# An expert layer's down weights, issued from the ScalarE queue instead of the SyncE queue

## What is computed

```
def block_ffn(args):
    xblk, e = args
    return (jax.nn.silu(xblk @ w_g[e]) * (xblk @ w_u[e])) @ w_d[e]

yb = lax.map(block_ffn, (xb, blk_e)).reshape(P, D)
```

## Time and profile before

| what | value |
|---|---|
| median of 3 runs | 4818.37 us (4810.97 to 4830.34) |
| time of the profiled execution | 4811.15 us |
| its span, first to last instruction | 4809.1 us |
| busy over the span: TensorE, VectorE, ScalarE, GpSimd | 76%, 37%, 19%, 1% |
| mean granted TensorE clock | 0.872 of full |
| bytes moved by DMA | 485.17 MB, mean 101 GB/s |
| experts' loads in it | 96 of 2048 KB each |
| first expert load issued, end of the last down product | 1516.03 us, 2041.70 us |

### The profile page before, as it was taken

The page is one execution under the profiler, slowest core; times in us unless marked ns, Lnnn a source line. Parts: engine busy times, 40 slices in busy tenths (PEclk is TensorE's granted clock), DMA queues, the critical chain, the costliest instruction groups (busy, mean ns, idle before and its releaser), DMA issues. The chain is left out here.

```text
span 4809.1 us, 70093 instructions
## 1 busy us (share of the span) xinstructions
PE 3634.8 (76%) x29962; PEld 2832.5 (59%) x29962; DVE 1793.0 (37%) x3421; ACT 924.6 (19%) x1532; POOL 54.4 (1%) x70
## 2 busy tenths in 40 slices
PE   4889959469964777738578655799989758778887
PEld 3678938347553344337238445688878645466677
DVE  4645543742242000054414245444410353344433
ACT  2154420122010111120001332211100212222211
POOL 0000000000000000000000000000000000000000
PEclk7989969789986999969689887899999879989888
DMA  4120006013414999934111000244420010012222
GB/s 150 42 101 4 4 30 180 13 46 97 131 62 177 423 423 423 391 106 133 41 44 62 3 1 27 59 113 118 120 77 25 24 38 1 18 49 70 66 64 81
DMA packets 376984, 485.17 MB, mean 101 GB/s; under 512 B 16311, under 2 KB 326104, under 8 KB 368513
## 3 DMA queue, kind: packets, MB, share of 16 engines
q1 hardware_dynamic: 367728, 459.59, 27.6%
q0 software_dynamic: 3856, 13.11, 0.7%
q10 hardware_dynamic: 5120, 8.39, 0.5%
HBM read 455.88 MB, written 25.18 MB: 100 GB/s over the span
## 5 line engine op out<-in xcount | busy, mean ns | idle before, releaser
L243 PE MATMUL banks<-leading,w_rest 128*128 128x512 f32 (+2 forms) x1920 | 716.1, 373 | 162.8 <-DVE w_rest L203 162.8
L243 PE MATMUL banks<-rest,w_leading 128*128 128x512 f32 (+2 forms) x1920 | 704.9, 367 | 0.0
L243 PE MATMUL banks<-leading,w_leading 128*128 128x512 f32 (+2 forms) x1920 | 703.1, 366 | 0.0
L243 PEld LDWEIGHTS banks<-leading,w_rest 128*128 128x128 f32 (+1 forms) x1920 | 374.4, 195 | 236.9 <-issue 97.2
L243 PE MATMUL banks<-w_rest,leading 128*128 128x256 f32 (+3 forms) x1332 | 395.3, 297 | 104.2 <-DVE w_rest L203 104.2
L203 DVE TENSOR_TENSOR w_rest<-w,w_leading 128x1024 fp32r<-128x1024 f32 (+4 forms) x304 | 280.8, 965 | 497.1 <-ACT w_leading L197 497.1
L243 PEld LDWEIGHTS banks<-leading,w_leading 128*128 128x128 f32 (+1 forms) x1920 | 374.0, 195 | 61.4
L243 PEld LDWEIGHTS banks<-rest,w_leading 128*128 128x128 f32 (+1 forms) x1920 | 375.0, 195 | 58.2
L197 ACT CAST w_leading<-w 128x1024 fp32r<-128x1024 f32 (+4 forms) x304 | 240.3, 838 | 846.6 <-DMA w<-in_w_in 458.3
L243 PE MATMUL banks<-w_leading,rest 128*128 128x256 f32 (+3 forms) x1332 | 390.7, 293 | 0.0
L243 PE MATMUL banks<-w_leading,leading 128*128 128x256 f32 (+3 forms) x1332 | 390.2, 293 | 0.0
(11 more groups left out here) (534 smaller groups left out, 4892.4 us busy)
## 6 DMA issues: line engine op xcount, KB each, us to landing
wg<-in_w_exp_gate SPq DMA_DIRECT2D x32, 2048.0 KB, 28.4
wu<-in_w_exp_up SPq DMA_DIRECT2D x32, 2048.0 KB, 28.4
wd<-in_w_exp_down SPq DMA_DIRECT2D x32, 2048.0 KB, 27.9
ws<-in_ada_w SPq DMA_DIRECT2D x96, 512.0 KB, 3.9
w<-in_w_in SPq DMA_DIRECT2D x41, 1024.0 KB, 5.4
w<-in_ffn_up SPq DMA_DIRECT2D x44, 512.0 KB
w<-in_ffn_up SPq DMA_DIRECT2D x88, 256.0 KB
ws<-in_w_ada SPq DMA_DIRECT2D x32, 512.0 KB, 3.9
```

The lines of the kernel that those rows point to most:

```text
L243: mm = nc.tensor.matmul(bank_of(r, kind, at), lhsT, rhs, start=(k == 0 and q == 0), stop=(k == kt - 1 and q == len(each) - 1))
```

## The change

The issue of the down weights leaves SyncE's loop. In ScalarE's loop it stands at the head of each block: a read of the block's expert, the same wait on `y_made_sem`, and the same DMA.

```
@@ -1753,8 +1753,6 @@
                         sp.dma_start(wg[u][:, :, :], a["w_exp_gate"][bass.ds(e, 1)].rearrange("o (p k) n -> p (o k) n", p=P)).then_inc(g_in_sem[u], 16)
                         sp.wait_ge(u_made_sem, 2 * it + u + 1)
                         sp.dma_start(wu[u][:, :, :], a["w_exp_up"][bass.ds(e, 1)].rearrange("o (p k) n -> p (o k) n", p=P)).then_inc(u_in_sem[u], 16)
-                        sp.wait_ge(y_made_sem, 2 * it + u + 1)
-                        sp.dma_start(wd[u][:, :, :], a["w_exp_down"][bass.ds(e, 1)].rearrange("o (k p) n -> p (o k) n", p=P)).then_inc(d_in_sem[u], 16)
 
             @block.gpsimd
             def _(pool):
@@ -1827,6 +1825,9 @@
                 with act.Fori(0, n) as it:
                     for u in range(2):
                         i = 2 * it + u
+                        e = act.value_load(m.expert_of[0:1, bass.ds(i, 1)], min_val=0, max_val=N_EXP - 1)
+                        act.wait_ge(y_made_sem, i + 1)
+                        act.dma_start(wd[u][:, :, :], a["w_exp_down"][bass.ds(e, 1)].rearrange("o (k p) n -> p (o k) n", p=P)).then_inc(d_in_sem[u], 16)
                         act.wait_ge(g_made_sem, i + 3)
                         nc.scalar.activation(b.sg[:, :], m.ps[:, 2, half(u)], ACT.Silu).then_inc(silu_sem, 1)
                         if u:
```

## The result

The changed kernel takes 5179.02 us (median of 4 runs, 5170.51 to 5186.12) against 4824.35 us for the kernel before (4 runs, 4810.97 to 4839.56). The ratio is 1.0737, 95% interval 1.0713 to 1.0762: 355 us slower. The forecast was 5147, with a range of 4950 to 5215.

The account below looks back on a forecast made before the run. The prediction took the experts to be bound by 16 full DMA engines. Its terms, 15.2 + 811.0 - 497.7 = 328.5 us, on the profiled 4811.15 us with 7.2 for the median, gave 5147 us, range 4950 to 5215.

Parts of the forecast that it names:

- The order on ScalarE puts the issue a block late: Head of ScalarE's block: load i issued only when block i-1 is finished, 3.06 us after the previous down product's last matmul.
- The first packets: Down load on ScalarE's queue: packets start 1.0 to 1.2 us after the issue, 1.2 taken, so at 4.26 us.
- When the gate and up loads arrive: Loads of block i+2 arrive at about 5 and 8.6 us, in the midst of the down load's transfer.
- All of both loads ahead of the down load: DMA engines: gate and up loads go through before the down load is done, 15.0 us for the three.
- One of the prediction's own signs of being wrong: Forecast is wrong if block i+2's gate and up loads land after block i's down load.
- Turns by the packet, whatever its size: DMA engines alternate queues packet by packet: 32 down turns against 16 larger packets; landing 18 us after issue; chance 0.80.
- Rival 1: DMA engines take longer turns or share by bytes: down load waits for one gate load, 4922 to 4991 us; chance 0.12.
- The down product at the lower clock: TensorE, idle some 12 us before it, takes 5.96 us instead of 3.65 for the down product.
- A block: Experts' stage, one block from down product to down product: 21.03 + 5.96 = 27.0 us instead of 16.13.
- The ends of the stage: First down product ends 15.2 us later; the last two blocks, without gate and up loads beside them, take 14.0 us each.
- Rival 2: Down load on its own queue is served at once, landing at 10.4 us; time stays at 4818 us; chance 0.04.
- Rival 3: Down load's issue meets busy engines, starts up to 4 us late: 116 us more, about 5260 us; chance 0.04.

Follow-up runs that it names:

- e11: Changed kernel with the value load ahead of the wait for y, issue still behind the stores, first down load ahead of all: 5082.15 us, ratio 1.0512 to the kernel before.
- e6: Changed kernel with value load ahead of the wait for y, issue ahead of the stores, first down load ahead of all: 4944.61 us; 62 us gain forecast, 234 measured.
- e3: Changed kernel with the down load in 8 packets of 16 KB per DMA engine instead of 32 of 4 KB: 4974.13 us, ratio 1.0292 to the kernel before.
- e5: Changed kernel with gate and up loads in 64 packets of 2 KB per DMA engine instead of 8 of 16 KB: 4949.08 us, ratio 1.0241 to the kernel before.
- e4b: Changed kernel with 26 extra matmuls into an unused bank ahead of TensorE's wait for the down load: 5137.84 us, ratio 1.0629 to the kernel before.
- e1: Changed kernel with the down load issued one block earlier, still on ScalarE's queue in 4 KB packets: 4900.86 us, ratio 1.0132 to the kernel before.

## Why the prediction was right, point by point

- **The order on ScalarE puts the issue a block late**: right. Issued 3.2 us after the previous down product, forecast 3.06.
- **The first packets** 1.2 us after the issue: right, some 1.0: issued at 1888.82, q10's packets run in the row that starts at 1889.6.
- **When the gate and up loads arrive**: wrong in size, about 5 and 8.6 us forecast. The gate load is issued at 3.6 and moves its first packets at 7.3 us, 3.6 us after the issue and not 1.2, and by then the engines are at work for q10. It left the sum alone, since in either case all of both loads goes through before the down load is done, but by a narrow margin and so in part by luck: 231 down packets, 14.4 per engine, were ahead of the gate load, not 5, and with over 16 the up load would no longer have been through, as in e11 and e6. The same mistake is why e6 came out at four times its forecast.
- **All of both loads ahead of the down load**: right to 3 packets. One of the prediction's own signs of being wrong, the up load landing after the down load, did come up, by a hair: in the block shown the down load lands at 1862.03 + 17.5 = 1879.5 and the up load at 1865.80 + 13.9 = 1879.7. In the next it is the other way round, 1907.9 and 1907.8. The load is waited for as forecast either way.
- **Turns by the packet, whatever its size**: right, 223 to 237 in the changed kernel, one for one from the gate load's first packets on, and e3 and e5 show that the packet size sets the time. Landing after 18.2 us, forecast 18. Rival 1 wanted 13 us, and falls with its sharing by bytes. Its longer turns were quoted from the Trainium skill (page "DMA: Bandwidth & Descriptors", section "Queues, rings and completion order"). The round robin there agrees with these rows. The length of the turn doesn't: that section has an engine drain a whole packet of typically 9 to 17 descriptors before it switches, and here it was one packet of the rows, as the half microseconds behind 1893.0 show. The landing alone would not have told: with turns of 8 or 9 packets the down load, with 18 left per engine, would also have let both loads through.
- **The down product at the lower clock**: 5.96 us forecast, 180.2 us / 32 = 5.63 measured. e4b gives it back, 2 us a block.
- **A block**: 27.0 forecast, 27.29 measured. 29 times 0.29 us are 8 of the 32 us by which the forecast was low.
- **The ends of the stage**: forecast 15.2 us for the first block; from the first load's issue to the end of the first down product it is 1558.91 - 1512.56 = 46.35 us, against 27.96 before: 18.4. The last two blocks took (2381.35 - 2350.39) / 2 = 15.5 us each, not 14.0; 1.7 of these 3 us are the first one's down product, 5.35 us at the lower clock. Together 6 us more. Stage 343 us against 328.5.
- **The rest**, 17 of the 32 us, lies outside the stage or in which runs are compared. Nothing in the change explains it; that stretch varies by as much between kernels that leave it alone, as said above, and why was not followed.
- Rival 2 (its own queue serves it at once) needed 70% of the engines; it had 86% for 3.3 us and then 19.8%. e6 comes near it, and even there a block takes 19.6 us. Rival 3 fell with the 1.0 us to the first packets.

## What to carry to other kernels

A load on a queue of its own overtakes the backlog of the other queue only at a packet for a packet, so small packets beside large ones get the small share; a load that is needed soon belongs ahead of the others in their queue, or on its own with packets as large as theirs, or clearly ahead of them in time. When a DMA's issue moves to a compute engine, read what that engine waits for just before it: here the wait for the previous block's result took away the block's lead that the double buffer had given. And where a stage is bound by DMA, a shorter time to landing proves nothing: it fell from 27.9 to 18.2 us while the stage grew by 343.

## What the runs showed of the hardware that I had not expected

- A load whose first packets fall into another queue's work moves nothing for 3.4 to 4.0 us (the gate loads of 28 blocks each of the changed kernel, e6 and e11), against about 1.0 on idle engines. It is the same the other way round: the changed kernel's first down load, issued at 1526.00 beside the backlog of q1, has its first packet after 3.7 us. What the wait is made of is not shown. Whoever is issued first thus keeps the engines alone for that long, and 2.3 us on the issue were worth 7.0 us a block.
- The 16 engines end a mixed load apart. The semaphore writes of the down load shown come within 0.6 us (1906.6 to 1907.2) in the changed kernel and within 3.6 us (1828.4 to 1832.0) in e11.
- Early is not enough: with two small-packet loads in line (e1) single landings took 40 us, with 14.7 us of waiting in every third block and none in the others. A mean over the blocks would have hidden that.
